# Mixing the values in the second layer's attention: values as stationary operand, two heads beside each other, no turning of the mixed heads

## The reference

```python
def stick_breaking_mixer(h, w_in, w_out):
    q, k, v = jnp.split(h @ w_in, 3, axis=-1)          # 16 heads of 64 each
    def sb_block(i0, i1):                               # blocks of 128 queries
        z = jnp.einsum('bqhd,bkhd->bhqk', q[:, i0:i1], k[:, :i1]) * scale
        mask = causal_mask(i0, i1, True)
        log_beta = jax.nn.log_sigmoid(z)
        log_keep = jnp.where(mask, jax.nn.log_sigmoid(-z), 0.0)
        later = lax.cumsum(log_keep, axis=3, reverse=True) - log_keep
        a = jnp.where(mask, jnp.exp(log_beta + later), 0.0)
        return jnp.einsum('bhqk,bkhd->bqhd', a, v[:, :i1])
    o = sweep_query_blocks(sb_block, seq)
    return o.reshape(bsz, seq, C_W) @ w_out

x = x + gate1 * mix                                     # then norm, route, experts
y = y + einsum('nef,efd->nd', hid * gate, w2[g])        # all 4 groups of 8 experts
```

## Time and profile before

| | us |
|---|---|
| median of 3 runs | 1314.98 (1314.77 to 1320.28) |
| the profiled execution, its own time | 1314.45 |
| its span in the profile | 1312.7 |
| PE busy | 922.8 (70%) |
| DVE busy | 292.4 (22%) |
| ACT busy | 204.0 (16%) |
| second layer's attention, first scores to last product of the output projection | about 729.6 to 841.5 |

### The profile page before, as it was taken

How to read it: one execution, slowest core, us unless ns; L and a number is a source line. 1 busy time by engine, 2 the same in 40 slices (tenths; PEclk the granted TensorE clock), 3 DMA queues, 4 the chain that set the end, 5 groups by cost and what they waited for, 6 DMA issues and landing times.

```text
span 1312.7 us, 13507 instructions
## 1 busy us (share of the span) xinstructions
PE 922.8 (70%) x5568; PEld 428.8 (33%) x5568; DVE 292.4 (22%) x596; ACT 204.0 (16%) x423; POOL 30.7 (2%) x89
## 2 busy tenths in 40 slices
PE   4999899556564737566779899976374665656485
PEld 1444555122221212122237666532121222213131
DVE  1535544011010101011026766421010110101011
ACT  2223324010110001000110453320010101010000
POOL 3000000000000000000000122000000000000000
PEclk9999998787788868688989998997786877877898
DMA  9984738899999999999999933599999999999995
GB/s 358 378 277 192 290 128 351 374 428 426 430 430 426 429 428 428 429 426 428 421 411 409 398 126 128 227 388 428 429 427 429 430 427 429 429 427 427 428 424 230
DMA packets 67575, 489.97 MB, mean 373 GB/s; under 512 B 18241, under 2 KB 18369, under 8 KB 37577
## 3 DMA queue, kind: packets, MB, share of 16 engines
q1 hardware_dynamic: 66832, 488.25, 89.8%
q10 hardware_dynamic: 696, 1.07, 0.2%
HBM read 488.25 MB, written 1.05 MB: 373 GB/s over the span
## 4 chain that ended last, share of the span: by engine, by line
DMA 51%; PE 41%; DVE 2%; SPq 2%; issue 1%; ACT 1%; DVEq 0%; ACTq 0%
DMA tokens<-in_moe_w_dram 45%; PE bank L927 12%; PE bank L688 8%; PE bank L956 5%; PE bank L840 4%; DMA ring<-in_mod_w_dram 4%; PE bank L728 4%; DMA ring<-in_moe_w_dram 2%; SPq L430 2%; PE bank L640 2%; DMA ring<-in_od_w_in_dram 1%; PE bank L780 1%; PE bank L796 1%; PE bank L896 1%; PE bank L675 1%
## 5 line engine op out<-in xcount | busy, mean ns | idle before, releaser
L927 PE MATMUL bank<-ring,region 128*32 128x512 f32 x1472 | 259.7, 666 | 168.2 <-DMA tokens<-in_moe_w_dram 83.4
L956 PE MATMUL bank<-ring,region 128*32 128x512 f32 x832 | 149.7, 748 | 149.2 <-DMA ring<-in_moe_w_dram 95.9
L927 PEld LDWEIGHTS bank<-ring,region 128*32 128x32 f32 x1472 | 69.0, 121 | 344.2 <-issue 279.3
L927 PE MATMUL bank<-work,region 128*32 128x512 f32 x256 | 130.5, 669 | 0.0
L927 PE MATMUL bank<-tokens,region 128*32 128x512 f32 x256 | 130.4, 669 | 0.0
L956 PEld LDWEIGHTS bank<-ring,region 128*32 128x32 f32 x832 | 39.2, 134 | 247.5 <-issue 211.8
L688 PE MATMUL bank<-ring,tokens 128*128 128x512 f32 x256 | 115.5, 603 | 2.7 <-ACT tokens L1127 2.7
L1751 DVE TENSOR_TENSOR region<-region,bank 128x512 f32<-128x512 f32 x16 | 11.0, 688 | 435.7 <-PE bank L927 435.7
L1758 DVE TENSOR_TENSOR region<-bank,region 128x512 f32<-128x512 f32 x32 | 20.6, 686 | 289.5 <-PE bank L956 289.5
L1127 ACT ACTIVATE region<-bank,shift,scale 128x128 f32<-128x128 f32 x64 | 24.1, 457 | 382.4 <-PE bank L914 382.4
L914 PE MATMUL bank<-region,h 128*128 128x128 f32 x512 | 63.4, 285 | 8.6 <-issue 7.8
(11 more groups left out here) (239 smaller groups left out, 906.8 us busy)
## 6 DMA issues: line engine op xcount, KB each, us to landing
ring<-in_moe_w_dram SPq DMA_DIRECT2D x144, 2048.0 KB, 19.4
ring<-in_mod_w_dram SPq DMA_DIRECT2D x23, 2048.0 KB, 14.7
work<-in_moe_w_dram SPq DMA_DIRECT2D x22, 2048.0 KB, 24.1
tokens<-in_moe_w_dram SPq DMA_DIRECT2D x22, 2048.0 KB, 28.5
ring<-in_ev_w_in_dram SPq DMA_DIRECT2D x6, 2048.0 KB, 19.5
ring<-in_od_w_in_dram SPq DMA_DIRECT2D x6, 2048.0 KB, 19.4
alone<-in_moe_w_dram SPq DMA_DIRECT2D x2, 2048.0 KB, 9.8
ring<-in_ev_w_out_dram SPq DMA_DIRECT2D x2, 2048.0 KB, 7.8
```

The lines of the kernel that those rows point to most:

```text
L927: last = pe.matmul(bank[which][32 * j:32 * j + 32, :], m.seated[:, k, 32 * j:32 * j + 32], weights(4 * which + j, k * FE), start=(k == 0), ...
L956: last = pe.matmul(bank[half][32 * j:32 * j + 32, :], m.hidT[:, c, 32 * j:32 * j + 32], w, start=(c == 0), stop=(c == FC - 1), skip_group_ ...
```

## The change

In layer 1, `mix_values` is replaced by `mix_pair`. It takes two neighbouring heads at once: 64 columns of v are the stationary operand and the turned attention weights `pT` are streamed (256 columns for the first 128 keys, 128 for the others). Head hh goes to the array's columns 0 to 63 and head hh + 1 to columns 64 to 127 (tile positions (0, 0) and (0, 64)), so the result lands with features on partitions and queries along the bank, which is the layout that `hT` wants. Four products for a pair instead of six. `mix_pair(hh - 2)` runs in the odd steps 5, 7, ..., 19, ahead of that step's transposes, where `mix_values` ran in every step from 4 to 19, behind them.

`copy_out`, `turn_half` and `copy_turned_half` are gone from layer 1. ACT copies both banks of the first half straight to `hT` in step 12 (`copy_mixed(0, 0)` and `(0, 1)`); of the second half DVE copies one bank and ACT the other. `project_out(1, 0, i)` moves from steps 14 to 17 to steps 13 to 16, right behind the modulation columns and ahead of `scores(1, 14)`, and waits for both copies. Layer 0 is left as it is; its functions only lose an argument.

```diff
--- before.py
+++ after.py
@@ -98,9 +98,9 @@
 PARTS = ({FIRST: 1, GATE1: 3, SECOND: 4, GATE2: 6}, {FIRST: 7, GATE2: 9})
 HT_STEPS = 12
 O_SQUARE_AT = 11
-O_READY_AT = (13, 12)
-O_TURN_AT = (14, 13)
-O_OUT_AT = (15, 14)
+O_READY_AT = 13
+O_TURN_AT = (14, 12)
+O_OUT_AT = (15, 13)
 QUAD_UNITS = 12
 EXPERT_UNITS = QUAD_UNITS * QUADS
 LAYER_UNITS = PE_UNITS[0] + EXPERT_UNITS
@@ -796,18 +796,18 @@
             last = pe.transpose(bank[2][:, i * P:(i + 1) * P], src[:, i * P:(i + 1) * P], m.ident[:, :])
         last.then_inc(s["p_turned"], 1)
 
-    def mix_values(l, w, n):
-
-        pe.wait_ge(s["pT_copied"], n + 1)
-        if l == 0 and w < 4:
+    def mix_values(w):
+
+        pe.wait_ge(s["pT_copied"], w + 1)
+        if w < 4:
             out, wide = w * 2 * HD, 2 * HD
         else:
-            out, wide = ((w - 4) * HD + COL if l == 0 else w * HD), HD
+            out, wide = (w - 4) * HD + COL, HD
         half, lo = divmod(out, COL)
-        if l == 0 and w == 0:
+        if w == 0:
             pe.wait_ge(s["cum_copied"], 2)
         if half == 1 and lo == 0:
-            pe.wait_ge(s["proj_copied"], TT * IN_UNITS * (l + 1))
+            pe.wait_ge(s["proj_copied"], TT * IN_UNITS)
         pT = m.pT[w % 2]
         o0, o1 = (bank[o_bank(half, t)][:, lo:lo + wide] for t in range(TT))
         v0, v1 = (m.v[:, t, out:out + wide] for t in range(TT))
@@ -816,11 +816,29 @@
         pe.matmul(o1, pT[:, 2 * P:3 * P], v1, start=False, stop=True, skip_group_check=True).then_inc(
             s["pv_done"], 1)
 
-    def turn_half(l, half):
+    def mix_pair(hh):
+
+
+        pe.wait_ge(s["pT_copied"], 12 + hh + 2)
+        if hh == NHH // 2:
+            pe.wait_ge(s["proj_copied"], TT * IN_UNITS * 2)
+        c = hh // 2 % 4
+        out = bank[o_bank(hh // 8, c // 2)][:, c % 2 * T:(c % 2 + 1) * T]
+        last = {}
+        for s_tile, lo, n in ((0, 0, T), (1, T, P)):
+            for i in range(2):
+                rows = slice(64 * i, 64 * i + 64)
+                last[i] = pe.matmul(out[rows, T - n:T], m.v[:, s_tile, (hh + i) * HD:(hh + i + 1) * HD],
+                                    m.pT[i][:, lo:lo + n], start=(s_tile == 0), stop=(s_tile == 1),
+                                    skip_group_check=True, tile_position=(0, 64 * i))
+        for i in range(2):
+            last[i].then_inc(s["pv_done"], 1)
+
+    def turn_half(half):
 
         for t in range(TT):
-            pe.wait_ge(s["o_ready"], 2 * TT * l + TT * half + t + 1)
-            o = m.normed[t][:, :] if l == 0 and half == 0 else m.h[:, t, half * COL:(half + 1) * COL]
+            pe.wait_ge(s["o_ready"], TT * half + t + 1)
+            o = m.normed[t][:, :] if half == 0 else m.h[:, t, half * COL:(half + 1) * COL]
             for c in range(4):
                 last = pe.transpose(bank[o_bank(half, t)][:, c * P:(c + 1) * P], o[:, c * P:(c + 1) * P],
                                     m.ident[:, :])
@@ -830,7 +848,7 @@
 
         t, u = divmod(i, OUT_UNITS)
         slot = full(l, OUT_AT[l][half])
-        pe.wait_ge(s["oT_copied"], 2 * TT * l + TT * half + (TT if i else 1))
+        pe.wait_ge(s["oT_copied"], 2 * TT * l + TT * half + (TT if i or l else 1))
         if half == 0 and i >= 2:
             pe.wait_ge(s["out_moved"], 8 * l + i - 1)
         if half == 1 and i < 2:
@@ -846,6 +864,8 @@
             if step < NHH and step % 2 == 0:
                 scores(l, step)
             hh = step - LAG[l]
+            if l == 1 and hh >= 2 and hh % 2 == 0:
+                mix_pair(hh - 2)
             w = weights_of(l, hh)
             if w is not None:
                 n = 12 * l + w
@@ -857,8 +877,8 @@
                     pe.wait_ge(s["prob_done"], 2 * (hh + 1))
                 turn_weights(l, w, m.pr[0 if l == 0 and w < 4 else hh % 2], n)
             w = weights_of(l, hh - 1)
-            if w is not None:
-                mix_values(l, w, 12 * l + w)
+            if l == 0 and w is not None:
+                mix_values(w)
             for i, part in LATE_PARTS[l].get(step, []):
                 project_item(l, i, (part,))
             if step < 2:
@@ -869,11 +889,12 @@
                 mod_cols(l, SECOND)
             if l == 0 and 2 <= step < 6:
                 turn_qk(step + 2)
-            if step == O_TURN_AT[l]:
-                turn_half(l, 0)
+            if l == 0 and step == O_TURN_AT[0]:
+                turn_half(0)
             if O_OUT_AT[l] <= step < O_OUT_AT[l] + 4:
                 project_out(l, 0, step - O_OUT_AT[l])
-        turn_half(l, 1)
+        if l == 0:
+            turn_half(1)
         for i in range(4):
             project_out(l, 1, i)
 
@@ -1074,6 +1095,16 @@
     return 2 if group == GATE1 else 2 + half
 
 
+def mixed_bank(bank, half, i):
+
+    return bank[o_bank(half, i)][:, :].rearrange("p (k t) -> p k t", k=2)
+
+
+def mixed_chunks(m, half, i):
+
+    return m.hT[:, 4 * half + 2 * i:4 * half + 2 * i + 2, :]
+
+
 def weights_of(l, hh):
 
     if not 0 <= hh < NHH:
@@ -1218,12 +1249,16 @@
         if l == 0 and 1 <= step <= 4:
             root8(step + 3)
 
-    def copy_turned_half(l, half):
+    def copy_turned_half(half):
         for t in range(TT):
-            act.wait_ge(s["oT_turned"], 2 * TT * l + TT * half + t + 1)
+            act.wait_ge(s["oT_turned"], TT * half + t + 1)
             fn(m.hT[:, 4 * half:4 * half + 4, t * P:(t + 1) * P],
                bank[o_bank(half, t)][:, :].rearrange("p (k t) -> p k t", k=4), ACT.Copy,
-               scale=m.sub_g[:, 0:1] if l == 0 and half == 0 else 1.0).then_inc(s["oT_copied"], 1)
+               scale=m.sub_g[:, 0:1] if half == 0 else 1.0).then_inc(s["oT_copied"], 1)
+
+    def copy_mixed(half, i):
+        act.wait_ge(s["pv_done"], 12 + 8 * (half + 1))
+        act.copy(mixed_chunks(m, half, i), mixed_bank(bank, half, i)).then_inc(s["oT_copied"], 1)
 
     def copy_weights(l, step):
 
@@ -1264,7 +1299,7 @@
             if step == O_SQUARE_AT + 1:
                 root8(8)
             if step == O_TURN_AT[0]:
-                copy_turned_half(0, 0)
+                copy_turned_half(0)
 
     def attend_odd():
         for step in range(NHH + LAG[1]):
@@ -1285,7 +1320,8 @@
                 fn(m.pr[hh % 2][:, :], m.normed[hh % 2][:, 0:ATT], ACT.Exp).then_inc(s["sb_exp"], 1)
             copy_weights(1, step)
             if step == O_TURN_AT[1]:
-                copy_turned_half(1, 0)
+                for i in range(2):
+                    copy_mixed(0, i)
 
     def route(l):
         copy_row(l, 2)
@@ -1338,7 +1374,10 @@
         else:
             project_early(1)
             attend_odd()
-        copy_turned_half(l, 1)
+        if l == 0:
+            copy_turned_half(1)
+        else:
+            copy_mixed(1, 1)
         norm(2 * l + 1)
         modulate(2 * l + 1)
         route(l)
@@ -1574,7 +1613,7 @@
                 norm_qk(step + 3)
             if step == O_SQUARE_AT + 1:
                 sum_squares()
-            if step == O_READY_AT[0]:
+            if step == O_READY_AT:
                 norm_heads()
         mod_cols(0, SECOND)
         add_first_half(0)
@@ -1623,18 +1662,14 @@
         dve.wait_ge(s["carry_ready"], 3)
         for step in range(NHH):
             break_stick(step)
-            if step == O_READY_AT[1]:
-                copy_out(0)
         mod_cols(1, SECOND)
         add_first_half(1)
-        copy_out(1)
+        copy_mixed(1, 0)
         add_out(1, 0, 3)
 
-    def copy_out(half):
+    def copy_mixed(half, i):
         dve.wait_ge(s["pv_done"], 12 + 8 * (half + 1))
-        for t in range(TT):
-            dve.tensor_copy(m.h[:, t, half * COL:(half + 1) * COL], bank[o_bank(half, t)][:, :]).then_inc(
-                s["o_ready"], 1)
+        dve.tensor_copy(mixed_chunks(m, half, i), mixed_bank(bank, half, i)).then_inc(s["oT_copied"], 1)
 
     def wait_out(l, half, i):
         if i < 3:
```

## The result

| | before | after |
|---|---|---|
| median of 20 runs, us | 1317.64 | 1321.68 |
| ratio to before | | 1.0029 (95% interval 1.0015 to 1.0043) |
| profiled execution, its own time / span | 1314.45 / 1312.7 | 1322.29 / 1320.5 |
| scores(4) to first output product of the second half | 77.04 | 82.95 |

The change makes the kernel slower, by 0.29%, some 4 us: less than the 0.5% that I took as the limit, but clear of zero with this many runs. The forecast was 0.7 us and a range of 1310 to 1320; the measured median lies above it. (Over its 20 runs the kernel before has 1317.64, where the first three alone had 1314.98, so 2.7 of the 6.4 us by which the absolute number is off belong to both kernels.) One of the 20 runs of the kernel before took 1406.05 us, a slow state that the ratio leaves out.

A forecast was written before the change was run, and what follows sets the result against it. Expert weight DMA bounds the kernel, but its full-rate start hangs on TensorE's attention chain. Chain terms put the second half 0.7 us later: 1314.45 + 0.7 = 1315.1, stated as 1315.3 us, range 1310 to 1320.

The forecast's parts named there:

- The mechanism that the prediction named as deciding: Before out 2, TensorE idles 4.6 us for DVE's first add_out, which needs heads 14 and 15 and so scores(14).
- the clock in steps 12 and 13: L653 runs at the full clock, 3.5 us instead of 4.20, and ends at 798.2 just as the clock falls.
- What a shift is worth at the end: A microsecond won or lost on TensorE between 750 and 841.5 us comes out as one at the end.
- Pairs: A mix_pair costs 1.0 us in TensorE's chain, like the scores, against 1.22 for two heads before.
- The cheap pair: Rival: halves run fully beside each other without switching cost, 0.66 us a pair, 1313.3 us in all; chance 0.12.
- the serial one: Rival: a pair's halves run one after the other, 1.5 us a pair, 1318.6 us in all; chance 0.10.
- Four pairs save 0.9: In steps 4 to 11 each of four pairs saves 0.22 us, so scores(12) starts 0.9 us earlier.
- ACT's copies in step 12 cost nothing: ACT's two new bank copies, 0.6 us each, are covered because DVE gets to head 13 later; uncovered 1.2.
- Tail: After out 3 the last heads' transposes and ACT's copies follow bare, with two waits of some 0.7 us.
- Clock low in out 2: After the idle wait out 2 runs at the low clock and loses 1.84 us, taking 5.3 us.
- Rows 8: Profile rows behind out 2's clock loss: after 5.23 us idle, 32 products took 5.48 us instead of 3.64.
- The slower rival: The clock stays low through out 2 and out 3, 7.0 us each: 9.5 us more, 1324.6 us; chance 0.06.

The follow-up runs named there:

- e1: Kernel before with only the output products out 0 to out 3 one step earlier, old mixing kept: ratio 1.0038.
- e8: Changed kernel with DVE's first two add_out moved early, behind break_stick(13) and break_stick(14): ratio 0.9966, stretch 72.07 us.
- e10: Changed kernel run again unaltered for a second profile: stretch 82.71 us.
- e2: Changed kernel with the output products one step later, back in steps 14 to 17: ratio 0.9962, stretch 72.62 us.
- e4: Changed kernel with five unread products in step 15, filling TensorE's wait before out 2: ratio 1.0000, stretch 80.35 us.
- e7: e2 with every pair's four products issued twice: ratio 1.0009, stretch 79.28 us.
- e3: Changed kernel with two unread products of 512 columns behind the transposes of step 12: ratio 1.0018, stretch 77.77 us.
- e5: Changed kernel with e2's later output products and e3's filling of step 12 together: ratio 0.9969, stretch 71.27 us.
- e9: e8 with the column sums L653 one step earlier, in step 12's idle time: ratio 0.9937, median 1309.63 us.

## Why the prediction was wrong

The mechanism that the prediction named as deciding was there, with its sizes: out 2 waits for DVE's multiply, 10.88 us after scores(14) (10.75 forecast), idle 4.83 (4.6). e1 and e8 show that it is the order of the two programs and nothing else. The failed step is the clock in steps 12 and 13: "at the full one it needs 3.5, and ends at 798.2, just as the clock falls". I took the moment of the fall from the kernel before as if it were fixed. In its place the runs showed the clock low from a point in pair 8 or L653 on wherever the idle time was left empty and L653 stood behind pair 8 (after, e10, e2, e4, e7, e8): in the changed kernel pair 8 took 1.26, L653 6.62 and out 0 6.22 us. In step 12 the kernel before mixed head 8 after the transposes and idled for 1.46 us; mix_pair takes that work out of the step, and the idle time is 1.98. That this thinner step is what brings the fall forward is likely by e3 and e5, but not shown beyond them, as the moment varies by 3 us with the order unchanged (table above).

By the prediction's own terms, in us of the stretch:

| term | forecast | measured | difference |
|---|---|---|---|
| scores(4) to scores(12), four pairs | -0.9 | -1.5 | -0.6 |
| pair 8 and transposes | 1.33 | 2.10 | +0.8 |
| L653 | 3.5 | 6.62 | +3.1 |
| out 0 | 5.19 | 6.22 | +1.0 |
| scores(14) to out 2 | 10.75 | 10.88 | +0.1 |
| out 2 | 5.3 | 6.27 | +1.0 |
| from its end to the second half | 8.8 | 8.6 | -0.2 |
| sum against before | +0.7 | +5.9 | +5.2 |

The five terms that grew add up to 6.0 us, 5.9 of them in products and transposes that ran at the low clock; 0.8 of gains elsewhere stand against them. e3 goes with it: with the idle time of step 12 filled, pair 8 takes 0.87, L653 3.5, and the stretch is 77.77 against the 77.7 of the sum (the rest of that match is two errors that cancel).

Point by point:
- *What a shift is worth at the end*: right behind the first expert slots, where the rest is constant within 2.5 us. "From there nothing differs but the shift" is not: from the second half to that release the changed kernel took 45.67 and 44.54 us, the kernel before 44.08 and 44.03, as the clock fell again at another time.
- *Pairs*: 1.0 forecast, 0.95 measured, split by e7 into 0.65 of streams and 0.30 of switching. The cheap pair (0.66) and the serial one (1.5) are both out.
- *Four pairs save 0.9*: 1.5. The mixing bound for 0.22 a pair gave 0.27, and beside that each projection part behind a pair or transposes takes 3.46 or 3.44 in place of 3.51 or 3.49; that smaller term I hadn't seen, and no run explains it.
- *ACT's copies in step 12 cost nothing*: right, DVE took up head 13 without a gap.
- *Tail*: two waits for ACT's copies, 0.66 and 0.57, as forecast.
- *Clock low in out 2*: right in kind, 2.8 us over the 3.49 of before and not 1.8. Rows 8 were an idle time of 5.23 us ahead of other products; e4 gives this one's price, 2.6.
- *The slower rival* (low clock through out 2 and out 3): not so, out 3 is at 3.44.
- *Range*: it had the clock's cost as one loss of 1.7 to 1.8, not as a longer low stretch in a region that the edit made thinner.

What stays open: the profiles differ by 5.9 us in the stretch and by 7.5 and 6.1 to the release, the medians of the runs by 4.0 (ratio 1.0029, 3.8 us). The times of the changed kernel lie near 1318 and near 1323; I have profiles of two of the slower kind only, and so can't show where the others are kinder. What moves the clock's fall from one execution to the next, with the same order ahead of it (e2, e8 against e4, e10), is open as well, and so is how much of the 4 us it makes up. That the column tiles of mix_pair count less for the clock than whole-array work wasn't tried by itself; e3 shows only that added work ahead of pair 8 is enough.

## What to carry to other kernels

Take a change of several edits apart by its orders first. Here the new mixing is worth 0.4% and the earlier output products, which looked like the harvest of it, cost more than that, since a product was put ahead of the scores that feed the longest chain, and behind an add that another engine does last. When you move work on one engine, look up where the other engines' programs release it, and move their instructions along. When an edit removes small work beside a wait, price what follows at the low clock: a thinner stretch can cost more than the work that was saved, and needed work put into the idle time (e9) is worth trying, though it isn't shown to beat e2 or e8. And follow a gain past the stretch in which it was made: e5's 1.3 us over e2 were gone at the release, as the clock fell once more on the way there and in e2's execution it didn't.

## What the runs showed of the hardware

- Added work made a stretch shorter: with 1.88 us of unread products it took 77.77 instead of 82.95 us (e3), as the granted clock stayed at its upper level (2.4 GHz) through the 32 one-column pieces behind them. On the other order the gain was 1.3 us (e5 against e2), and the moment of the fall varied by 3 us for the same work ahead of it.
- The part between the second half and SP's release took 42.85 us with the clock never low (e2), 44.0 to 44.5 with it low for about 3.4 us, and 45.5 to 45.8 with it low for 6.3 to 6.8.
- Going from whole-array products to half-width column tiles and back cost 0.30 us, 0.15 each way (e7); two column halves stream fully beside each other (0.65 us for 0.66).
- Behind an idle time of 4.83 us on TensorE the next eight products took 6.27 us; with 4.46 us of unread work in it they took 3.67 (e4), and with no idle time ahead 3.43 (e8).
